# Mixing layers of a fused two-block transformer: the last gate pair as seven block products, and the output projection's contraction steps in another order

## The reference, cut to what matters

```python
for l in range(DEPTH):                      # DEPTH = 2
    h = rms_norm(x, ln_mix_pre[l])
    z = h @ w_in[l]
    z_q, z_kv, z_g, z_ret, z_rwkv, z_conv, z_gate = split_cols(z, IN_SIZES)
    ...                                     # four branches of 256 channels each
    gates = jax.nn.sigmoid(z_gate).reshape(B, S, N_BRANCHES, D_MODEL)
    branches = (o_nsa, o_ret, o_rwkv, o_conv)
    merged = gates[:, :, 0] * (branches[0] @ w_branch[l, 0])
    for m in range(1, N_BRANCHES):
        merged = merged + gates[:, :, m] * (branches[m] @ w_branch[l, m])
    x = x + rms_norm(merged @ w_mix_out[l], ln_mix_post[l])
    ...                                     # cross attention, MLP
```

## Time and profile before

| what | value |
|---|---|
| median of 3 runs | 2736.48 us (2736.4 to 2738.21) |
| the profiled execution | 2736.28 us, span 2734.4 us |
| TensorE busy | 2675.0 us, 98% |
| VectorE, ScalarE, GpSimd busy | 1705.1, 472.0, 102.3 us |
| mean granted clock of TensorE | 0.998 of full speed |

### The profile page before, as it was taken

The page is one execution under the profiler, slowest core; times in us unless marked ns, Lnnn a source line. Parts: engine busy times, 40 slices in busy tenths (PEclk is TensorE's granted clock), DMA queues, the critical chain, the costliest instruction groups (busy, mean ns, idle before and its releaser), DMA issues.

```text
span 2734.4 us, 48316 instructions
## 1 busy us (share of the span) xinstructions
PE 2675.0 (98%) x20672; PEld 2053.7 (75%) x20672; DVE 1705.1 (62%) x2998; ACT 472.0 (17%) x933; POOL 102.3 (4%) x134
## 2 busy tenths in 40 slices
PE   8999999999999999999999999999999999999997
PEld 6789887776688879777776787556777777777775
DVE  3654464776355437477654764246778778778776
ACT  2220212101222121200142111220111111111111
POOL 0011300000001220000000000000000000000000
PEclk9999999999999999999999999999999999999999
DMA  6321443443333243444343433339999999999995
GB/s 271 121 110 71 177 153 120 175 185 155 108 131 124 78 175 118 170 170 177 126 153 123 170 154 137 138 132 425 424 387 421 399 392 412 423 396 409 423 420 238
DMA packets 59293, 621.29 MB, mean 227 GB/s; under 512 B 6720, under 2 KB 7104, under 8 KB 10944
## 3 DMA queue, kind: packets, MB, share of 16 engines
q1 hardware_dynamic: 55008, 602.25, 55.3%
q0 software_dynamic: 2720, 13.52, 1.2%
q10 hardware_dynamic: 1344, 2.36, 0.2%
HBM read 614.70 MB, written 3.41 MB: 226 GB/s over the span
## 4 chain that ended last, share of the span: by engine, by line
PE 83%; DVE 9%; DMA 6%; issue 1%; ACT 1%; SPq 0%; DVEq 0%; ACTq 0%
PE ps L810 11%; PE ps L1379 10%; PE ps L1748 9%; PE ps L1391 8%; PE ps L1232 7%; PE ps L1768 6%; PE ps L852 5%; DMA slabA<-in_od_exp_w 4%; PE ps L1210 4%; PE ps L1783 4%; PE ps L1823 2%; PE ps L791 2%; PE ps L1244 2%; DMA fbT<-in_od_exp_w 2%; PE ps L1357 1%; PE ps L897 1%
## 5 line engine op out<-in xcount | busy, mean ns | idle before, releaser
L1768 PE MATMUL ps<-fbT,work 128*64 128x256 f32 x1792 | 205.8, 382 | 6.7 <-DMA fbT<-in_od_exp_w 6.7
L1232 PE MATMUL ps<-hT,slabA 128*128 128x256 f32 x832 | 188.9, 380 | 1.1 <-ACT work L2096 1.1
L1768 PEld LDWEIGHTS ps<-fbT,work 128*64 128x64 f32 x1792 | 123.7, 137 | 74.0 <-DMA fbT<-in_od_exp_w 9.4
L1232 PEld LDWEIGHTS ps<-hT,slabA 128*128 128x128 f32 x832 | 155.7, 190 | 23.4 <-ACT work L2096 1.9
L1748 PE MATMUL ps<-prm,hT 128*64 128x128 f32 x2592 | 162.6, 274 | 8.2 <-DVE resets L3358 8.0
L810 PE MATMUL ps<-hT,slabA 128*128 128x256 f32 x736 | 163.4, 381 | 0.0
L1748 PEld LDWEIGHTS ps<-prm,hT 128*64 128x64 f32 x2592 | 146.3, 136 | 20.1 <-DVE resets L3358 11.3
L2412 DVE TENSOR_TENSOR work<-work 128x256 f32<-128x256 f32 (+2 forms) x201 | 81.1, 403 | 127.4 <-ACT work L2068 98.3
L1379 PEld LDWEIGHTS ps<-work 128*128 128x128 f32 x1152 | 139.5, 192 | 21.5 <-issue 21.0
L810 PEld LDWEIGHTS ps<-hT,slabA 128*128 128x128 f32 x736 | 138.3, 190 | 20.5 <-issue 2.5
L1379 PE MATMUL ps<-work 128*128 128x128 f32 x1152 | 143.9, 275 | 0.1
(11 more groups left out here) (513 smaller groups left out, 4639.5 us busy)
## 6 DMA issues: line engine op xcount, KB each, us to landing
slabA<-in_od_exp_w SPq DMA_DIRECT2D x56, 2048.0 KB, 12.9
fbT<-in_od_exp_w SPq DMA_DIRECT2D x56, 2048.0 KB
slabB<-in_od_exp_w SPq DMA_DIRECT2D x56, 1024.0 KB, 12.4
fbT<-in_od_exp_w SPq DMA_DIRECT2D x56, 1024.0 KB, 13.3
slabA<-in_w_in SPq DMA_DIRECT2D x24, 2048.0 KB, 8.1
slabA<-in_mlp_w SPq DMA_DIRECT2D x16, 2048.0 KB, 9.3
slabB<-in_mlp_w SPq DMA_DIRECT2D x32, 1024.0 KB, 4.8
slabA<-in_ev_ffn_w SPq DMA_DIRECT2D x11, 2048.0 KB, 7.7
```

The costliest lines, as they stand in the source:

```text
L1232: last = mm(ps[:, b, 0:T], side["gates"][:, k, c % 4 * P:(c % 4 + 1) * P], hT[:, k, :], start=(k == 0), stop=(k == KD - 1))
L1768: last = mm(ps[SMALL * j:SMALL * (j + 1), 1, 0:2 * P].rearrange("p (w n) -> p w n", w=2), xs[:, k, :], v[:, k, :, j * P:(j + 1) * P], star ...
```

## The change

The pair that begins at unit 30 is added to `gate_pairs`, and the two plain units at the end go. The slab of units 28 to 31 is given up with the last block product, and later counts of `proj_ready` are adapted. The four blocks of the output projection are no longer done one after the other: steps 0 to 4 of blocks (0,0), (0,1) and (1,0) come first, then steps 5 to 7 of the same three, then block (1,1) whole. The waits for the sums of the last columns move with step 5, 6 and 7 of block (0,0).

```diff
-        gate_pairs = (24, 26, 28)
+        gate_pairs = (24, 26, 28, 30)
...
-                        ringA.load(sp, [cols(w, IN_SLABS, GATE0 + m * D + half * 512)], groups(4) if (i, half) == (3, 0) else None)
+                        ringA.load(sp, [cols(w, IN_SLABS, GATE0 + m * D + half * 512)], groups(4) if i == 3 else None)
...
-                of_last_gates, of_first_slab = 2, 2
-                ringA.load(sp, [cols(a["xa_wkv"][l], slabs_of(2 * D), 512)], groups(of_last_gates + of_first_slab + 4))
+                of_first_slab = 2
+                ringA.load(sp, [cols(a["xa_wkv"][l], slabs_of(2 * D), 512)], groups(of_first_slab + 4))
...
-                if u > gate_pairs[-1]:
-                    pe.wait_ge(sem("proj_free"), due("pe", "proj_free"))
-                elif u >= PROJ:
+                if u >= PROJ:
                     pe.wait_ge(sem("side_gate"), due("pe", "side_gate"))
...
-                for u in range(4 * KD - 2, 4 * KD):
-                    side_gate(u)
-                for u in range(4 * KD - 2, 4 * KD):
-                    side_branch(u)
...
-                        pe.wait_ge(sem("proj_free"), due("pe", "proj_free"))
-                        pe.wait_ge(sem("side_gate"), due("pe", "side_gate", 2 * len(gate_pairs) + 2))
-                rows_out(merged, column=merged_columns)
+                        pe.wait_ge(sem("proj_free"), due("pe", "proj_free", PROJ))
+                        pe.wait_ge(sem("side_gate"), due("pe", "side_gate", 2 * len(gate_pairs)))
+                slabs = []
+
+                def sums_out(t, half, ks):
+                    if half == len(slabs):
+                        slabs.append(kview(ringA.take(pe), 512))
+                    for k in ks:
+                        if not t and not half:
+                            merged_columns(k)
+                        last = mm(ps[:, 4 + 2 * t + half, :], merged[:, k, t * P:(t + 1) * P], slabs[half][:, k, :], start=(k == 0), stop=(k == KD - 1))
+                    return last
+                early, late = range(KD - 3), range(KD - 3, KD)
+                for t, half in ((0, 0), (0, 1), (1, 0)):
+                    sums_out(t, half, early)
+                sums_out(0, 0, late)
+                sums_out(0, 1, late).then_inc(sem("rows_psum"), up("rows_psum"))
+                sums_out(1, 0, late).then_inc(sem("slabA_used"), up("slabA_used"))
+                sums_out(1, 1, range(KD)).then_inc(sem("rows_psum"), up("rows_psum"))
...
-                side_gates(2)
+                side_gates(0)
```

## The result

| | before | changed |
|---|---|---|
| median of 19 runs | 2737.0 us | 2742.72 us |
| range | 2733.68 to 2739.06 us | 2739.59 to 2748.23 us |
| ratio, 95% interval | | 1.0019 (1.0013 to 1.0025) |
| span of the profiled execution | 2734.4 us | 2740.4 us |

A forecast was written before the change was run, and what follows sets the result against it. TensorE, busy 98% of the span, was taken to bound the kernel. Per layer -0.66 + 2.49 and -0.66 + 2.42 gave +3.6 us in all, forecast 2740.0 us, range 2737.0 to 2743.4.

The forecast's parts named there:

- Part one: End of the gate units: seven block products replace two plain units, 6.25 for 6.91 us, gaining 0.66 us per layer.
- Part two: Second half of w_mix_out: issued 0.66 us earlier, landing 8.1 and 8.0 us after issue, at 330.21 and 999.75.
- Part three: Output projection order: block (0,1) reached before its slab lands, stalling TensorE 2.49 and 2.42 us, hiding a 0.1 us wait.
- What follows behind: After the projection: first token rows complete later, but second rows are not delayed and everything behind moves with TensorE.
- The clock: TensorE's clock falling to its lower level after the projection stall, 1.7 us per fall; chance 0.22.
- rival (a): Clock falls in the projection stall: 2741.7 us with one fall, 2743.4 with two; chance 0.22, two thirds with one.
- likeliest case: Whole kernel: the forecast itself, stalls without a clock fall, 2739 to 2741.5 us; chance 0.58.

The follow-up runs named there:

- order-alone kernel: New order of the output projection alone, last two gate units plain as in the kernel before: 2743.01 us, ratio 1.0023 against the kernel before.
- 4 and 6 early steps: Changed kernel with 4 or 6 early contraction steps per block in place of 5: 2743.87 us (1.0025) with four, 2739.14 us (1.0006) with six.
- pair-only kernel: Fourth gate pair added to the kernel before, output projection in its old order: 2736.0 us (0.9991), measured again 2737.19 us (0.9999).

## Why the prediction was right

**Part one** held: 6.91 us of plain units became 6.26 us of block products, no wait in them. VectorE's sums were ready at 312.5 us, for 312.9 forecast, and the third product that needs them began at 317.8.

**Part two** held: the slab landed 8.26 and 7.98 us after its issue, for 8.1 and 8.0 taken from the same transfer of before.

**Part three** held, and it is where the sum is decided: stalls of 2.49 and 2.42 us forecast, 2.47 and 2.20 measured, and 2.18 and 2.67 when the changed kernel was measured again. How near the first of these came is in part luck. The forecast let 0.22 us pass between the landing and the matmul, taken from a place where nothing waited; behind a landing it is 0.04 us (the piece called issue in the chain), and in the first layer a landing 0.16 us later than forecast made up for it. The order-alone kernel shows that it is this part and nothing else; 4 and 6 early steps that the gap goes with the number of records ahead of block (0,1). The wait hidden in return was forecast at 0.1 us and is 0.25. In the pair-only kernel GpSimd's last sum ends at 329.39, 6.10 us behind the projection's start at 323.29, and 6.11 was forecast; the forecast set this end against the matmul of step 7 and left out the weight load between them, which starts at 329.45. That the load makes up the rest of the 0.25 us is argued from these times, not tested.

**What follows behind** held: the late first token rows cost nothing.

**The clock** is the one term that was mis-sized. It stood as rival (a) with a chance of 0.22, and the likeliest case had none of it. The step that failed is "It decides from an idle time somewhere between 2.16 and 2.54 us", drawn from two rows. The trace of before already spoke against it. There the clock also falls behind an idle time of 0.92 us, which the prediction doesn't mention:

```profile
1830.14 2.33 PE L1697 MATMUL ps<-cst 128*128 128x128 f32 x10 [0.92 <-issue]
...
1830.00:1834.00 4.00, 3.86 (x17) 3.87 (x18) 1.90 (x8) 1.49 (x2) 0.00 (x0) 0.57 0.86 274
```

Ten gaps of 1.8 to 3.1 us in the projection, from five kernels, show five falls, and no length that divides them:

| idle before block (0,1), us | 1.79 | 2.01 | 2.03 | 2.09 | 2.09 | 2.31 | 2.36 | 2.51 | 2.80 | 3.13 |
|---|---|---|---|---|---|---|---|---|---|---|
| clock fell | no | yes | no | no | no | yes | yes | yes | yes | no |

Four of the five falls lie among the five longest gaps, but the longest has none. They also sort by place: four falls came in the first layer's five gaps and one in the second's five. No run separates the place from the length, so what decides stays open. An expected cost would have been the right form. With the share of gaps that fell, known only now, it is 2 gaps x 0.5 x 1.6 us = 1.6 us, and the sum is +3.6 + 1.6 = +5.2 us, as the ratio says; the interval from 3.6 to 6.8 us is too wide to confirm the 1.6 us by itself.

The median of 2742.72 us lies above the 2741.5 at which the likeliest case ended and between the 2741.7 and 2743.4 us of rival (a), so the range holds it thanks to that rival. The forecast point was 2740.0, and 2.1 of the 2.7 us between are accounted for: 1.6 by the clock, 0.5 by a median of before that was itself 2737.0 in 19 runs for 2736.48 in three. The likeliest outcome, with 0.78, was no change beyond 0.2%, up to 2742.0. By the ratio, 0.19%, it came; by the median itself it is passed by 0.7 us. That it fell on this side is luck. One smaller sum was off: with the stalls of 1.2 us that the prediction worked out for a landing in 6.8 us, the time is 2737.4 to 2737.6, not 2737.3.

## What to carry to other kernels

Before reordering work to hide one wait, list every wait that the reordered instructions carry, and find for each when its releaser comes: here 0.25 us of waiting for sums was hidden by pulling a wait for a transfer forward by 2.6 us, when a weight load of the trace already began at the moment of landing. When several pieces of work are free to fill a gap, take first those that read what is already there; (1,0) before (0,1) costs nothing and takes both waits away. And price a hole of 2 us in TensorE's stream above its length, since it may cost the clock as well.

## What the runs showed of the hardware

- A fall of the clock behind a gap costs 1.4 to 1.7 us here (24.88 to 25.14 us for 54 records instead of 23.44, 26.00 for 24.30 with 56), and whether it comes is not decided by the idle time alone: 3.13 us without one, 2.01 us with one. The kernel before shows one behind 0.92 us. In the kernel with 4 early steps it fell behind an idle time of 1.90 us elsewhere (L791, at 1441.98), where the granted clock of the next 3.6 us was 0.59; the same wait of 1.90 us left it alone in the kernel before.

```profile
1441.90:1445.50 3.60, 3.52 (x12) 2.90 (x13) 0.03 (x1) 1.66 (x6) 0.00 (x0) 0.59 0.02 5
```

- The second half of w_mix_out (2 MB) took 7.7 to 8.5 us from issue to landing in all these kernels; two loads with nothing queued right behind them took 8.3 and 8.0 us, the same two with 2 MB more behind them 8.26 and 7.98. What comes later in the same queue didn't delay what was ahead. The Trainium skill, "DMA: Bandwidth & Descriptors", section "Anatomy of one DMA", has about 2 us plus the bytes over 436 GB/s for a transfer issued by GpSimd, 6.8 us for this size as an estimate. These loads are issued by SyncE and took 0.9 to 1.7 us longer, at 389 to 397 GB/s in the windows above.
